# A decoder block in float32 on one core: gate/up pairs as seven products of quarters, and one square kept in PSUM

## What is computed

```
xn = RMSNorm(x);  P = xn @ W_in + b_in        # gMLP u|v, GLA q|k|v|r|low-rank, two branch gates
A  = gelu(u) * (W_s LN(gelu(v)) + b_s)        # 8 groups, 128-position chunks
B  = chunked gated linear attention, 4 heads, per-head RMSNorm, swish(r)
h  = x + (sigmoid(ga) * A W_a + sigmoid(gb) * B W_b) @ W_out
xn2 = RMSNorm(h)
h  = h + (silu(xn2 @ w_gate) * (xn2 @ w_up)) @ w_down      # D_FF = 2816 = 11 * 256
y  = RMSNorm(h) * final_w
```

## Time and profile before

| | |
|---|---|
| runs, median | 869.38 us |
| the profiled execution | 869.42 us, its span 867.7 us |
| PE busy | 848.8 us (98% of the span), 4014 matmuls |
| PE weight loads | 708.8 us (82%), beside the matmuls |
| POOL, ACT, DVE busy | 337.9, 314.8, 310.9 us (36 to 39%) |
| DMA | 89.8 MB, mean 104 GB/s |
| granted TensorE clock, mean | 0.997 |

### The profile page before, as it was taken

One profiled execution on the slowest core, in us unless ns is written; L12 is line 12 of the kernel. 1 busy time (PEld: TensorE's weight loads), 2 busy tenths in 40 slices (PEclk: granted clock), 3 DMA queues, 4 the chain that ended last, 5 costly groups with the idle time before them and its releaser, 6 DMA issues.

```text
span 867.7 us, 10234 instructions
## 1 busy us (share of the span) xinstructions
PE 848.8 (98%) x4014; PEld 708.8 (82%) x4014; DVE 310.9 (36%) x305; ACT 314.8 (36%) x313; POOL 337.9 (39%) x80
## 2 busy tenths in 40 slices
PE   8999999999999999999999999999999999999996
PEld 7888888777877888888888798888888888888885
DVE  6464337675675721212121333000000000444445
ACT  3532445754755523232321552222222222222233
POOL 4444433224224243434344425444444444444440
PEclk9999999999999999999999999999999999999998
DMA  8742212122112122222235212222222222222212
GB/s 322 274 175 83 100 61 97 54 92 97 48 48 97 49 97 97 97 97 97 97 100 215 97 50 97 97 97 97 97 97 97 97 97 97 97 97 97 97 48 97
DMA packets 14658, 89.82 MB, mean 104 GB/s; under 512 B 1712, under 2 KB 1968, under 8 KB 5296
## 3 DMA queue, kind: packets, MB, share of 16 engines
q1 hardware_dynamic: 12384, 82.32, 26.0%
q10 hardware_dynamic: 2256, 7.24, 2.4%
HBM read 87.46 MB, written 2.10 MB: 103 GB/s over the span
## 4 chain that ended last, share of the span: by engine, by line
PE 90%; DVE 4%; ACT 2%; issue 1%; DMA 1%; POOL 0%; DVEq 0%; ACTq 0%; POOLq 0%
PE bank L863 19%; PE bank L865 19%; PE bank L864 19%; PE bank L881 9%; PE bank L882 9%; PE bank L880 9%; DVE osq L729 1%; DVE vgs L654 1%; PE bank L1017 1%; PE bank L1022 1%; PE bank L1009 1%; DMA par<-cols 1%; PE bank L1029 1%; PE bank L909 0%; ACT w_hi L309 0%
## 5 line engine op out<-in xcount | busy, mean ns | idle before, releaser
L262 POOL TENSOR_TENSOR w_lo<-raw,w_hi 128x2048 fp32r<-128x2048 f32 x71 | 327.1, 4607 | 479.7 <-ACT w_hi L309 479.7
L863 PE MATMUL bank<-xt_hi,w_hi 128*128 128x512 f32 (+1 forms) x704 | 269.1, 382 | 1.9 <-DVE xt_lo L565 1.0
L865 PE MATMUL bank<-xt_hi,w_lo 128*128 128x512 f32 (+1 forms) x704 | 267.1, 379 | 0.0
L864 PE MATMUL bank<-xt_lo,w_hi 128*128 128x512 f32 (+1 forms) x704 | 267.1, 379 | 0.0
L309 ACT ACTIVATE w_hi<-raw 128x2048 fp32r<-128x2048 f32 x72 | 137.7, 1912 | 297.3 <-PE bank L865 157.1
L863 PEld LDWEIGHTS bank<-xt_hi,w_hi 128*128 128x128 f32 x704 | 132.4, 188 | 28.8 <-issue 3.7
L864 PEld LDWEIGHTS bank<-xt_lo,w_hi 128*128 128x128 f32 x704 | 132.4, 188 | 25.2
L865 PEld LDWEIGHTS bank<-xt_hi,w_lo 128*128 128x128 f32 x704 | 132.4, 188 | 25.0
L804 DVE TENSOR_TENSOR act<-bank,sil 128x512 f32 (+1 forms) x22 | 15.2, 692 | 199.2 <-PE bank L865 199.2
L809 DVE TENSOR_TENSOR al<-act,ah 128x1024 fp32r<-128x1024 f32 x11 | 51.7, 4701 | 60.2 <-ACT ah L507 60.2
L880 PE MATMUL bank<-w_hi,ah 128*128 128x512 f32 x176 | 68.5, 389 | 0.0
(11 more groups left out here) (182 smaller groups left out, 943.7 us busy)
## 6 DMA issues: line engine op xcount, KB each, us to landing
raw<-wstream SPq DMA_DIRECT2D x72, 1024.0 KB, 4.8
xw<-x_t SPq DMA_DIRECT2D x4, 512.0 KB, 8.2
h<-x ACTq DMA_DIRECT2D x1, 2048.0 KB, 7.8
out<-h SPq DMA_DIRECT2D x3, 512.0 KB, 2.6
raw<-wstream SPq DMA_DIRECT2D x2, 512.0 KB, 5.9
xn_in<-x SPq DMA_DIRECT2D x2, 512.0 KB, 12.0
xn_in<-x ACTq DMA_DIRECT2D x2, 512.0 KB, 4.2
vbias_bc<-vbias ACTq DMA_DIRECT2D x1, 1024.0 KB, 8.2
```

Of the source, the lines that this page charges most:

```text
L262: pool.tensor_tensor(w_lo[s][:, :], raw[s][:, :], w_hi[s][:, :], ALU.subtract).then_inc(lo_ready, 1)
L863: pe.matmul(dst, wh[:, k, cs], rh[:, k, ts], start=(k == 0), stop=False)
L864: pe.matmul(dst, wh[:, k, cs], rl[:, k, ts], start=False, stop=False)
L865: last = pe.matmul(dst, wl[:, k, cs], rh[:, k, ts], start=False, stop=(k == KD - 1))
```

## The change

**Gate/up pairs.** The first pair stays as it is. The ten others are each computed with seven products of quarters instead of eight (the Winograd form of Strassen's scheme). A pair's weights (1024 x 256, for gate and for up) and `xt` (1024 x 512) are cut in two along both axes. With A the weights (first index: columns 0-127 or 128-255; second: k-tiles 0-3 or 4-7) and B = `xt` (first index: k-tiles; second: tokens 0-255 or 256-511):

The core of the diff, by engine. POOL, steady pair and what follows the last one:

```diff
+            def pair(p, c, first=False, last=False):
+
+                a12_low(c, at(p, 7, 4 - 7))
+                if not first:
+                    gated_pair((p[0], p[1] - 1))
+                a22_low(c, at(p, 7, 6 - 7))
+                if not last:
+                    a11_low(1 - c, at(p, 7, 1))
+
+            a11_low(0, 1)
...
+            pool.wait_ge(product_done, 7 * PAIRS - 3)
+            low(B_DOWN, 0, 8 * B_DOWN + 16)
+            gated_pair((None, PAIRS))
+            low(B_DOWN + 1, 1, 8 * B_DOWN + 16)
```

ACT: the square, what precedes the pairs, a pair, and what follows:

```diff
+                a.wait_ge(state_ready, i * 3 + 3)
                 a.wait_ge(o_done, i * 2 + 1)
-                a.activation(osq[:, :], bank[6][:, :], ACT.Square).then_inc(sq_ready, 1)
+                a.activation(bank[5][:, :], bank[6][:, :], ACT.Square).then_inc(sq_ready, 1)
...
+            a21_copy(0, 16)
+            t_split(0, tb_hi[0][:, :, :])
+            a11_high(0, 16)
+            s_high("S1", chain, 1)
+            t_split(1, tb_hi[1][:, :, :])
+            gate(0)
+            gate(1)
+            t_split(2, tb_hi[2][:, :, :])
+            a.wait_ge(up_done, 2)
+            s_high("S3", diff, 2)
+            a12_high(0, 16)
+            s_high("S2", chain, 3)
+            t_split(3, xt_hi[:, 0:4, HT:SEQ])
...
+                if not first:
+                    a.wait_ge(product_done, at(p, 7, -7))
+                    s_high("S2", chain, at(p, 4, 3 - 4))
+                take_p1(p, first)
+                if not first:
+                    pair_silu((p[0], p[1] - 1))
+                a.wait_ge(product_done, at(p, 7, 2 - 7))
+                a22_high(c, n)
+                a.wait_ge(product_done, at(p, 7, 3 - 7))
+                s_high("S4", chain, at(p, 4))
+                if not last:
+                    a.wait_ge(s_low, at(p, 4, 1 - 4))
+                    a21_copy(1 - c, nn)
+                    a11_high(1 - c, nn)
+                take_c11(p, first)
+                if not last:
+                    a.wait_ge(product_done, at(p, 7, 6 - 7))
+                    s_high("S1", chain, at(p, 4, 1))
+                    s_high("S3", diff, at(p, 4, 2))
+                    a12_high(1 - c, nn)
...
             act_high(0, 0)
...
+            a.wait_ge(pair_ready, 1)
             act_high(1, 1)
+            a.wait_ge(plain_low, 3 * PAIRS)
+            high2(B_DOWN, 0, s_formed, 4 * PAIRS)
+            high2(B_DOWN + 1, 1, s_formed, 4 * PAIRS)
+            pair_silu((None, PAIRS))
```

DVE:

```diff
-                v.tensor_tensor(osq[:, :], osq[:, :], rs[:, :], ALU.add).then_inc(osq_ready, 1)
+                v.tensor_tensor(osq[:, :], bank[5][:, :], rs[:, :], ALU.add).then_inc(osq_ready, 1)
...
+            def form_s2(c):
+                v.tensor_tensor(chain, chain, wp[c][:, :, 0:4, 0:P], ALU.subtract).then_inc(s_formed, 1)
...
+            def s_low_of(name, src, high):
+                v.wait_ge(op_high, high)
+                v.tensor_tensor(op_lo[name][:, :, :, :], src, op_hi[name][:, :, :, :], ALU.subtract).then_inc(s_low, 1)
...
+            v.tensor_tensor(tf[0][:, :, :], b12, b11, ALU.subtract).then_inc(t_formed, 1)
+            form_s1(0, 16, 1)
...
+            v.tensor_tensor(tf[1][:, :, :], b22, tf[0][:, :, :], ALU.subtract).then_inc(t_formed, 1)
+            t_low_of(0, tb_lo[0][:, :, :], tb_hi[0][:, :, :])
+            s_low_of("S1", chain, 2)
+            form_s3(0)
...
+            form_s2(0)
+            v.tensor_tensor(tf[2][:, :, :], b22, b12, ALU.subtract).then_inc(t_formed, 1)
...
+            first_gated(0)
+            first_gated(1)
+            t_low_of(1, tb_lo[1][:, :, :], tb_hi[1][:, :, :])
...
+            v.tensor_tensor(tf[3][:, :, :], b21, tf[1][:, :, :], ALU.subtract).then_inc(t_formed, 1)
+            s_low_of("S3", diff, 3)
+            t_low_of(2, tb_lo[2][:, :, :], tb_hi[2][:, :, :])
+            s_low_of("S2", chain, 5)
+            t_low_of(3, xt_lo[:, 0:4, HT:SEQ], xt_hi[:, 0:4, HT:SEQ])
...
+            form_s4(0)
...
+                if not first:
+                    form_s2(c)
+                    join_c12((p[0], p[1] - 1))
+                    s_low_of("S2", chain, at(p, 7, 5 - 7))
+                    v.wait_ge(s_low, at(p, 4, 3 - 4))
+                    form_s4(c)
+                join_u2(p)
+                s_low_of("S4", chain, at(p, 7))
+                if not last:
+                    v.wait_ge(s_low, at(p, 4))
+                    form_s1(1 - c, nn, at(p, 1, 1))
+                join_u3(p)
+                join_c22(p, first)
+                if not last:
+                    form_s3(1 - c)
+                join_c21(p)
+                if not last:
+                    s_low_of("S1", chain, at(p, 7, 2))
+                    s_low_of("S3", diff, at(p, 7, 3))
+                    v.wait_ge(s_low, at(p, 4, 1))
...
             act_low(0, 0)
...
             act_low(1, 1)
+            join_c12((None, PAIRS))
```

PE, the first three products of a pair (of seven):

```diff
+            def pair(p, first=False):
+
+
+                pe.wait_ge(op_high, p * 7 + (1 - 7))
+                pe.wait_ge(plain_low, p * 3 + (1 - 3))
...
+                    pe.wait_ge(taken, p * 2 - 2)
+                product("A11", x11, 0, True)
+
+                pe.wait_ge(s_low, p * 4 + (1 - 4))
...
+                    pe.wait_ge(joined, p * 5 - 5)
+                product("S1", t1, 2, True)
+
+                pe.wait_ge(s_low, p * 4 + (3 - 4))
...
+                product("S2", t2, 1, True)
```

More of the change, by code:

```diff
@@ L492, in _ @@
             normalise_h(3)
[L493 to L501, removed]
-                    a.activation(sil[:, t, :], bank[t][:, :], ACT.Silu).then_inc(sil_ready, 1)
-                high2(i * 2 + (B_FFN + 2), 0, gate_done, i * 2 + 2)
-                high2(i * 2 + (B_FFN + 3), 1, up_done, i * 2 + 2)
+            split_turned(2)
@@ new lines, in a11_high, with a12_high, a22_high, s_high @@
+            def a11_high(c, n):
+                plain_high("A11", c, slice(0, 4), slice(0, P), k1_landed, n)
+            def a12_high(c, n):
+                plain_high("A12", c, slice(4, 8), slice(0, P), k2_landed, n)
+            def a22_high(c, n):
+                plain_high("A22", c, slice(4, 8), slice(P, 2 * P), k2_landed, n)
+            def s_high(name, src, formed):
+                a.wait_ge(s_formed, formed)
+                a.activation(op_hi[name][:, :, :, :], src, ACT.Copy).then_inc(op_high, 1)
@@ new lines, in quarter, with join_c22, join_c21 @@
+            def quarter(n, b, u):
+                return v.tensor_tensor(cq[:, n, :, :], bank[b][:, :].rearrange("p (g t) -> p g t", g=2),
+                                       u[:, :].rearrange("p (g t) -> p g t", g=2), ALU.add)
+            def join_c22(p, first=False):
+                if not first:
+                    v.wait_ge(pair_ready, at(p, 1, -1))
+                v.wait_ge(joined, at(p, 5, 2 - 5))
+                quarter(3, 2, u3).then_inc(joined, 1)
+            def join_c21(p):
+                v.wait_ge(product_done, at(p, 7, 6 - 7))
+                quarter(2, 3, u2).then_inc(joined, 1)
@@ new lines, in join_c12, with pair @@
+            def join_c12(p):
+                v.wait_ge(product_done, at(p, 7))
+                quarter(1, 2, u2).then_inc(joined, 1)
+            def pair(p, c, nn, first=False, last=False):
+                if not first:
+                    form_s2(c)
[17 more added lines that the diff above has]
+                    v.wait_ge(s_low, at(p, 4, 1))
@@ new lines, in _, with product @@
+            x21 = (xt_hi[:, 4:8, 0:HT], xt_lo[:, 4:8, 0:HT])
+            x22 = (xt_hi[:, 4:8, HT:SEQ], xt_lo[:, 4:8, HT:SEQ])
+            t1, t2, t3 = ((tb_hi[n], tb_lo[n]) for n in range(3))
+            t4 = (xt_hi[:, 0:4, HT:SEQ], xt_lo[:, 0:4, HT:SEQ])
+            def product(name, x, b, start):
+                wh, wl = op_hi[name], op_lo[name]
+                for g in range(2):
+                    dst = bank[b][:, g * HT:(g + 1) * HT]
+                    for k in range(4):
+                        pe.matmul(dst, wh[:, g, k, :], x[0][:, k, :], start=(start and g == 0 and k == 0), stop=False,
+                                  skip_group_check=True)
+                        pe.matmul(dst, wh[:, g, k, :], x[1][:, k, :], start=False, stop=False, skip_group_check=True)
+                        mm = pe.matmul(dst, wl[:, g, k, :], x[0][:, k, :], start=False, stop=(k == 3),
+                                       skip_group_check=True)
+                mm.then_inc(product_done, 1)
@@ L1096, in down @@
+            pair(1, True)
+            with pe.Fori(2, PAIRS + 1) as p:
+                pair(p)
             def down(m, s, first=False, last=False):
```

273 lines of the change are left out of this document (200 added, 73 removed).

## The result

The changed kernel takes **854.14 us** (median of 4 runs, 853.36 to 855.0), the kernel before 869.36 (869.32 to 869.48) beside it: a ratio of 0.9825, 95% interval 0.9813 to 0.9837. A later batch of five runs gave 854.84. Forecast were 851.6 us, with 849.5 to 859.5. A few single runs of the study lie 2 to 11 us above their neighbours at a lower mean clock (0.978 to 0.993); they stand in the medians and intervals given, no reading rests on them, and since no profile caught one, their cause stays open.

A forecast was written before the change was run, and what follows sets the result against it. TensorE, busy for 98% of the span, was taken to bound the kernel. From 869.42 us, 10.6 us came off for the pairs with entry and exit holes and 7.2 for the heads: 851.6 us, range 849.5 to 859.5.

The forecast's parts named there:

- The pairs on TensorE: Ten pairs: 168 matmuls at 0.120 us, 20.16 us a pair in place of 21.75, saving 15.9 us if TensorE never waits.
- Rival (d): Pairs: short matmuls cost half a long one, 19.0 us a pair, 11 us more gained, 840 us; chance 0.01.
- the 0.109 us by the rule of the Trainium skill: Pairs: 6 + N cycles a matmul, 0.109 us for the short width; they would save 23.8 us, not 15.9.
- (b): Pairs: waits between products cost TensorE time at seven boundaries a pair, 5 to 14 us, 857 to 866; chance 0.07.
- Operands beside TensorE: Steady pairs: DVE, POOL and ACT keep up, C12 0.24 us before wanted; cost zero, upper bound 0.5 us a pair.
- Rival (a): Steady pairs: C12 comes late, each pair but the first loses 0.3 to 0.6 us, 855 to 857; chance 0.22.
- The heads: Four heads: the add takes 0.69 us with one input in a bank, 1.80 us less each, 7.2 us in all.
- Entry: First of the ten pairs: S2's product waits for its low part, a hole of 2.2 us, bounds 0 and 4.
- Exit: Before the first down block: TensorE waits for POOL's weight split, a hole of 4.0 us, bounds 3.5 and 5.

The follow-up runs named there:

- run 9: Changed kernel with one more DVE operation between forming S2 and joining C12 in nine pairs: 857.59 us.
- run 10: Changed kernel with C12 joined ahead of the forming of S2 in nine pairs: 854.99 us.
- run 11: Changed kernel with the sums `chain` and `diff` in SBUF instead of PSUM banks 4 to 7, output not the block's: 876.07 us.
- run 2: Changed kernel with unread matmuls filling both holes, 20 before S2's product in the first of the ten pairs and 14 before the first down block: 852.04 us.
- run 3: Changed kernel with the splits for the first down block moved into the last pair, so the exit's hole goes: 849.58 us.
- run 4: The exit reordering of run 3 on the changed kernel, plus the low part of S2 ahead of T3's at the entry: 847.23 us.
- run 6: Changed kernel with only the low part of S2 moved ahead of T3's at the entry, the exit's hole left: 852.2 us.
- the control: The changed kernel run again with no edit: 854.84 us.
- run 5: Run 4's kernel with u3 joined right behind u2 in the first of the ten pairs: 845.96 us.

## Why the prediction was right or wrong

**The pairs on TensorE**: right. 0.120 us a matmul, 20.16 us a pair as forecast. Rival (d) and the 0.109 us by the rule of the Trainium skill are out, and so is (b): the starts go on at 0.12 us across products with their waits.

**Operands beside TensorE, zero in the steady pair**: right, and for the reason given. C12 ended 5.34 us after A22 in the first of the nine pairs and 5.42 in the next (forecast 5.37), in time; runs 9 and 10 show that the room was real and small. The reading from one row (L804 at 0.69 us within a POOL instruction) that one input in a bank frees DVE from POOL carried the whole forecast; run 11 shows the other side of it. Rival (a) did not come about.

**The heads**: right. 1.80 us in the first head as worked out; 7.56 us at the end of the first pair, 7.7 in a kernel with nothing else changed. The 0.4 us above the four heads' 7.2 are the restart: without a wait ahead of it the pair of ones matmuls takes 1.02 us in place of 1.12, and 4 x (1.80 + 0.10) = 7.6.

**Entry**: the mechanism was right in its order (A12's low part, then T3's, then S2's), the size 2.71 us for 2.2. POOL held to 6.19 us after the first pair's end, where I had 5.53, and that came from further up. I had the first pair's weights landed by about 511.5, 11.2 us before that end, in time for S1. In fact the forming of S1 stood for 1.16 us until they came, at 505.51, 9.65 us before the end of the first pair. DVE's row was then late all the way: T3 was formed 0.46 us after that end and not before it, T4 at 3.93 us for 3.23, and POOL, held up by T4's two SBUF inputs, began and ended 0.7 us later.

**Exit**: right. 3.63 us for 4.0, ended by POOL, which had asked before the second `al`.

**The term that was missing** stood in no step. The sum priced the two holes at their length, and took the matmuls behind them at the old pace. They ran at half clock for a while: 1.70 us at the entry, 1.71 at the exit (1.80 by the length of the down part). With it: 851.6 + 3.4 + 0.5 - 0.4 - 0.4 = 854.7, against 855.0 for the profiled execution; the other 0.3 us lie outside the profile's span. The loss is shown by rows, and that it hangs on the holes by runs 2, 3 and 4 and the count of profiles in run 6. The kernel before had given no warning that could be priced: its largest holes near here, 1.63 us and 1.04, were followed by the full clock. That holes of 2.2 and 4.0 us lie outside what those rows cover was a reason to bound this cost too; the prediction gave it no bound.

That the result fell in the range was luck. The median of 854.14 lies just inside the 854.5 that I had allowed for wide holes at entry and exit, but the two holes together were only 0.1 us longer than forecast; the profiled 855.0 lies inside only through the allowance for (a), which did not occur. In both cases that room was taken by a cost that the prediction did not name.

## What to carry to other kernels

On a kernel that TensorE bounds at 98%, list each hole that a change opens with its length, and add to the longer ones the half clock behind them (here 1.7 us each, in all seven profiles behind 3.6 us, at times behind 1.6 to 2.7); reorder the one instruction that is waited for, or let TensorE do matmuls in it that nobody reads, and then look for what is late next. Where DVE and POOL work side by side, count the SBUF inputs of each DVE operation: one operand in a PSUM bank saved 2.0 us on one add and some 20 us over the pairs. A tight order is tested by delaying it: one operation of 0.60 us told the room that was left. And a pace is read over several steps: single distances between equal points of neighbouring pairs go from 20.07 to 20.17 us.

## What the runs showed that I had not expected

TensorE's clock fell to its lower level behind short holes in an otherwise full stream. Behind 2.7 us idle it fell in some executions (the changed kernel's profile) and not in others (the control's); behind 3.6 us it fell in all seven profiles that have such a hole, though a single run 1.5 us under the others (850.67 in run 6) suggests that it need not. With the sums in SBUF two of nine holes of 1.8 us brought it about, and the other seven did not. Behind the hole of about 1.6 us at 10 us it fell in one profile only, that of run 3. After holes of 1.63 us in the heads and 1.0 us in run 4 the granted clock stayed at 1.00. In the changed kernel and in run 6 the missing clock added up to 1.70 or 1.71 us each time. So the length of a hole alone doesn't decide, and what else does stays open. It makes a kernel's runs fall into groups that lie that far apart, and the versions without the two holes (runs 4 and 5) repeat within 0.3 us, but for one run.

A second surprise is that useless matmuls pay: in run 2 TensorE did 34 more and the kernel was 2.8 us faster. The start after a wait, too, was not as charged: TensorE starts 0.06 us after the end of the DVE operation (I had 0.15; 178.78 after 178.72 in the earlier trace rows shows the 0.06 already), and the next matmul comes 0.10 us late (I had 0.07).
